# Entry of a gated delta net reordered, and its row scalings spread from DRAM

## The reference

```
q = l2_normalize(q) * 128 ** -0.5;  k = l2_normalize(k)
gcum  = cumsum(g)                                  # in a chunk
decay = exp(gcum_i - gcum_j), causal
m     = strict(k_beta k^T * decay)
u, w  = solve(I + m, [v * beta, k_beta * exp(gcum)])
attn  = (q k^T) * decay
q_dec = q * exp(gcum)                              # the row scaling of the queries
for each chunk:  v_new = u - w S;  o = q_dec S + attn v_new
                 S = S * exp(g_last) + k_dec^T v_new
```

## Time and profile before

| | before |
|---|---|
| runs (us) | 1338.09, 1340.19, 1348.91 |
| median | 1340.19 |
| profiled execution | 1343.36, span 1341.6 |
| PE busy | 1304.7 us, 97% of the span |
| DVE, ACT, POOL busy | 64%, 51%, 22% |
| mean granted TensorE clock | 0.991 |
| chain that ended last, by engine | PE 77%, DVE 10%, ACT 5% |

### The profile page before, as it was taken

How to read it: one execution, slowest core, us unless ns; L and a number is a source line. 1 busy time by engine, 2 the same in 40 slices (tenths; PEclk the granted TensorE clock), 3 DMA queues, 4 the chain that set the end, 5 groups by cost and what they waited for, 6 DMA issues and landing times.

```text
span 1341.6 us, 27229 instructions
## 1 busy us (share of the span) xinstructions
PE 1304.7 (97%) x10946; PEld 1226.9 (91%) x10946; DVE 859.0 (64%) x1271; ACT 681.5 (51%) x1098; POOL 290.8 (22%) x368
## 2 busy tenths in 40 slices
PE   6999999999799999999999999999999999999998
PEld 4899999997688888999999999999999988999998
DVE  4754789995457666533677656666736666875663
ACT  4458888866555554322534212343236665664553
POOL 3000223412587897513000000000130000200002
PEclk8999999999899999999999999999999999999999
DMA  9722323244231111123466566565423321556662
GB/s 325 209 80 81 94 79 95 80 114 151 98 111 33 49 48 33 64 95 110 146 202 196 181 193 195 183 197 178 129 95 126 97 69 32 182 173 220 190 201 80
DMA packets 138926, 174.90 MB, mean 130 GB/s; under 512 B 11025, under 2 KB 121873, under 8 KB 138561
## 3 DMA queue, kind: packets, MB, share of 16 engines
q1 hardware_dynamic: 137312, 168.94, 39.9%
q10 hardware_dynamic: 896, 4.23, 0.9%
q0 software_dynamic: 608, 0.19, 0.1%
HBM read 172.25 MB, written 1.08 MB: 129 GB/s over the span
## 4 chain that ended last, share of the span: by engine, by line
PE 77%; DVE 10%; ACT 5%; issue 3%; POOL 2%; DMA 1%; SPq 0%; ACTq 0%; DVEq 0%; POOLq 0%
PE bank L2728 54%; PE bank L2736 4%; DVE w_lo L1778 3%; DVE qkv L1864 2%; PE bank L3132 2%; PE bank L3141 2%; ACT w_hi L951 1%; PE bank L2654 1%; POOL qkv L806 1%; PE bank L3087 1%; PE bank L3408 1%; PE bank L3431 1%; DMA first_w<-in_w_mod 1%; PE bank L3006 1%; PE bank L3074 1%
## 5 line engine op out<-in xcount | busy, mean ns | idle before, releaser
L1778 DVE TENSOR_TENSOR w_lo<-raw,w_hi 128x1024 fp32r<-128x1024 f32 x212 | 264.2, 1247 | 297.1 <-ACT w_hi L951 296.6
L951 ACT ACTIVATE w_hi<-raw 128x1024 fp32r<-128x1024 f32 x212 | 223.9, 1057 | 379.9 <-PE bank L2728 371.8
L2728 PE MATMUL bank<-h_hi,w_hi 128*128 128x256 f32 x1472 | 299.4, 282 | 5.4 <-DVE w_lo L1778 2.9
L2728 PE MATMUL bank<-h_hi,w_lo 128*128 128x256 f32 x1472 | 293.7, 278 | 0.0
L2728 PE MATMUL bank<-h_lo,w_hi 128*128 128x256 f32 x1472 | 288.3, 278 | 0.0
L2728 PEld LDWEIGHTS bank<-h_hi,w_hi 128*128 128x128 f32 x1472 | 225.8, 189 | 15.5 <-issue 10.0
L2728 PEld LDWEIGHTS bank<-h_hi,w_lo 128*128 128x128 f32 x1472 | 225.7, 189 | 0.0
L2728 PEld LDWEIGHTS bank<-h_lo,w_hi 128*128 128x128 f32 x1472 | 222.6, 188 | 0.3 <-DVE h_lo L2076 0.2
L2728 PE MATMUL bank<-hid_hi,w_hi 128*128 128x256 f32 x768 | 172.0, 278 | 0.0
L2728 PE MATMUL bank<-hid_lo,w_hi 128*128 128x256 f32 x768 | 170.8, 277 | 0.0
L2728 PE MATMUL bank<-hid_hi,w_lo 128*128 128x256 f32 x768 | 170.7, 277 | 0.0
(11 more groups left out here) (380 smaller groups left out, 2445.3 us busy)
## 6 DMA issues: line engine op xcount, KB each, us to landing
raw<-in_mlp_w SPq DMA_DIRECT2D x128, 512.0 KB, 3.6
late_w<-in_w_mod SPq DMA_DIRECT2D x56, 512.0 KB, 4.4
raw<-in_even_w_in SPq DMA_DIRECT2D x48, 512.0 KB, 3.7
raw<-in_w_mod SPq DMA_DIRECT2D x24, 512.0 KB, 4.3
first_w<-in_w_mod SPq DMA_DIRECT2D x16, 512.0 KB, 11.2
raw<-in_even_w_out SPq DMA_DIRECT2D x16, 512.0 KB, 3.5
raw<-in_attn_w_qkv SPq DMA_DIRECT2D x16, 512.0 KB, 3.5
raw<-in_attn_w_o SPq DMA_DIRECT2D x8, 512.0 KB, 3.5
```

Source lines behind the costliest of these rows:

```text
L951: act.activation(stored(w_hi, j, four), raw[:, j % RAW], ACT.Copy).then_inc(hi_ready, 1)
L1778: dve.tensor_tensor(stored(w_lo, j, four), raw[:, j % RAW], stored(w_hi, j, four).bitcast(F32), ALU.subtract).then_inc(split_done, 1)
L2728: return pe.matmul(bank[2 * pair + t][:, c - n0:c - n0 + CTX], w_[:, k, t * P:(t + 1) * P], x_[:, c:c + CTX], start=(kk == 0 and first and ...
```

## The change

The row scalings come from a DRAM scratch. In body 8 ACT also writes exp of the gate sums of all steps to `eg_tok`, PE turns it (one transpose of 128 by 64), ACT copies the 64 by 128 result and stores it to `eg_rows`. ACT then loads, for each step, two transfers that put four rows of 128 on all partitions of `d_qd`. PE's and ACT's `rows` are gone, `log_gates` waits for `decay` (`p_dc`) instead, `decayed_q` for the transfers. The scratch of `eg_tok` and `eg_row` shares memory with `near`, hence the wait for `s_egw` there.

The entry is reordered: DVE leaves the wait for the silu of body 8's second pair until after `l2_scaled(1)`, and the split of unit 2 goes behind that; ACT loads group 2 before it takes the root of group 3, with the table load ahead of `neighbours`; PE starts step 0 when group 2 is scaled, not group 3; `decay(1)` moves ahead of the first doubling; DVE's split of an output unit in step 0 goes behind `neighbours(1)`.

```diff
@@ POOL
             def log_gates(q, d):
                 if q:
-                    pool.wait_ge(p_row, 2 * q - d)
+                    pool.wait_ge(p_dc, q)
...
             def decayed_q(q):
-                pool.wait_ge(a_row, 2 * q + 2)
+                pool.wait_ge(s_eg, 32 * (q + 1))
@@ ACT, the last two bodies of the input projection
                 if ends:
+                    act.preload_act_table_set("natural_log_exp_and_others")
                     neighbours(0)
-                    act.preload_act_table_set("natural_log_exp_and_others")
+                    l2_load(2)
                     l2_rstd(3)
-                    l2_load(2)
...
                     act.preload_act_table_set("silu_and_others")
                     evac(s, it, 1)
-                    act.preload_act_table_set("natural_log_exp_and_others")
...
                     l2_rstd(0)
                     act.wait_ge(s_gps, 3)
+                    eg_ = bank[X2][:, 0:64].rearrange("p (n d h) -> p n d h", d=2, h=8)
+                    for d in range(2):
+                        for cp in range(2):
...
+                            act.activation(y_, x_.rearrange("p c (g a) -> p g c a", a=2), ACT.Exp)
...
                     l2_rstd(1)
+                    act.wait_ge(s_gps, 4)
+                    act.activation(eg_row[0:8 * STEPS, :], bank[X0][0:8 * STEPS, 0:P], ACT.Copy).then_inc(s_gate, 1)
+                    act.wait_ge(s_gate, 7)
+                    act.dma_start(eg_dram[:, :], eg_row[0:8 * STEPS, :]).then_inc(s_egw, 16)
                     betas(0)
                     decay(0)
                     l2_load(1)
@@ ACT, the delta net
-            def rows(q, d):
-
-                act.wait_ge(p_row, 2 * q + 2 - d)
-                if q >= 2:
-                    act.wait_ge(p_os, q - 1)
-                act.activation(flat(d_qd[q % 2][:, d]), bank[R0][:, :], ACT.Exp).then_inc(a_row, 1)
...
+            def row_loads(q):
+                if q == 0:
+                    act.wait_ge(s_egw, 16)
+                    act.wait_ge(act_evac, 16)
+                else:
+                    act.wait_ge(g_qd, q)
+                if q >= 2:
+                    act.wait_ge(p_os, q - 1)
+                for d in range(2):
+                    r_ = 8 * q + 4 * d
+                    act.dma_start(d_qd[q % 2][:, d].rearrange("p i x -> p (i x)"),
+                                  eg_dram[r_:r_ + 4, :].rearrange("r x -> (r x)").partition_broadcast(P)).then_inc(s_eg, 16)
+
             flipped(0, -1, 0)
-            rows(0, 0)
             flipped(0, -1, 1)
+            act.preload_act_table_set("natural_log_exp_and_others")
+            row_loads(0)
             for q in range(STEPS):
...
                 gathered(q, 2, 1)
                 if prep:
-                    rows(q + 1, 1)
+                    row_loads(q + 1)
...
@@ DVE, entry and step 0
                     for part in range(3):
                         neighbours(0, part)
+                    l2_scaled(1)
+                    evac(s, it - 1, 1)
                     split_lo(u + 2, 2)
-                    l2_scaled(1)
...
-                evac(s, it, 1)
+                if b != LRU_TILES:
+                    evac(s, it, 1)
...
                 scores(q)
-                if q == 0:
-                    split_lo(SEG["out"]["unit"] + 1, 1)
                 masked(q, 2, 0)
                 reduced(q, 1, 1)
                 if prep:
                     neighbours(q + 1, 1)
                     neighbours(q + 1, 2)
+                if q == 0:
+                    split_lo(SEG["out"]["unit"] + 1, 1)
@@ PE
-            def rows(q, d):
...
-                for g_ in (d_gu, d_gl):
-                    mm = pe.matmul(bank[R0][:, :], lines[:, 2], flat(g_[:, d]), start=g_ is d_gu, stop=g_ is d_gl)
-                mm.then_inc(p_row, 1)
...
                     if g == 1:
                         pe.wait_ge(s_gate, 6)
+                        pe.wait_ge(l2["rs"], 1)
+                        pe.transpose(bank[X0][0:8 * STEPS, 0:P], eg_tok[:, :], C("ident")).then_inc(s_gps, 1)
                         decay(0)
...
-            pe.wait_ge(l2["out"], L2_OUT[3])
+            pe.wait_ge(l2["out"], L2_OUT[2])
...
-                if prep and q:
+                if prep:
                     decay(q + 1)
...
-                if prep and q == 0:
-                    decay(1)
...
                 second_product(q, 2, 1)
-                if prep:
-                    rows(q + 1, 1)
...
                 flip(q, 2, 1)
-                if prep:
-                    rows(q + 1, 0)
```

More of the change, by code:

```diff
@@ L3168, in l2_sums @@
                 pe.wait_ge(l2["sq"], 2 * g + 2)
+                if g == 2:
+                    pe.wait_ge(s_gate, 7)
                 if g >= 2:
@@ L3225, in _ @@
             first_product(0, 0, 0)
-            rows(0, 1)
             flip(0, -1, 0)
-            rows(0, 0)
             for q in range(STEPS):
```

21 lines of the change are left out of this document (12 added, 9 removed).

## The result

Over 20 runs each, the changed kernel takes 1335.91 us (1333.47 to 1343.31) and the kernel before 1344.8 us (1338.09 to 1349.99): a ratio of 0.9936, interval 0.9923 to 0.9948, or 8.6 us less (7.0 to 10.4). Faster, within 1%, as forecast to be likeliest; but the gain is smaller than the forecast 13.1 us, and 1335.91 lies just above the range of 1321 to 1335.

A forecast was written before the change was run, and what follows sets the result against it. The prediction took a chain of waits to bound the entry, and PE and an equally long circle through other engines the steps: 10.7 + 1.3 + 1.1 = 13.1 us off 1340.19, giving 1327.1 us, range 1321 to 1335.

The forecast's parts named there:

- The entry: Before step 1's decays: a chain of waits shortened by the new order, decays at 341.9 instead of 351.00, 9.1 us.
- the 2.9 taken: Entry: time assumed for POOL's pair of `d_t`, between 2.48 and 4.31 us in earlier rows.
- The 3.7: Entry: `d_t` time if DVE's lock on the shared port blocks POOL for one split; the sum would fall by 0.8 us.
- Step 0: From step 1's decays to `spread(1)`: further gains of 1.1 and 0.5 us, making 10.7 us with the entry.
- the split: Step 0: DVE's 1.57 us split moved behind the work for which PE waited, 1.1 us.
- PE's slow stretch at 359.55: Step 0: PE's 1.22 us there would become the 0.70 of a later step, 0.5 us.
- The steps: Row products removed from PE: 1.3 us in three even steps plus 1.1 in the last, 2.4 of 7.7 us.
- the last step: Last of the steps: no gates to write and no next decay, so its row products count in full, 1.1 us.
- Late transfers: Rival: POOL's copy of `d_last` waits for slow loads; gain gone at 12.4 us landing, 1353 at 14.4; chance 0.04.
- The rival with all row products: Rival in the steps: all 7.7 us of row products count, 18.4 us in total, 1321.8; chance 0.12.
- The filler's weights: Step 0: weight piece 3 waits for the moved split; PE may stand up to 1.6 us, taken as 0, bounds 0 and 0.5.
- the clock could take gain: Rival in the steps: PE's granted clock falls from 2.4 to 1.2 GHz; 26 us of it eats the gain; chance 0.03.

The follow-up runs named there:

- p_after: The changed kernel run again unaltered, as the measure for other runs of its call; ratio to the kernel before 0.9938 (0.9922 to 0.9954).
- c_dummy1: The changed kernel with matmuls of the row products' size and number put back on PE, 1.1 us per step; ratio to the kernel before 0.9937.
- e_spread: The changed kernel with one of seven levels of GpSimd's `spread` left out in steps 1 to 7; ratio to the kernel before 0.9888.
- d_dummy2: The changed kernel with twice the row products' matmuls put back on PE, 2.2 us per step; ratio to the kernel before 0.9962.

## Why the prediction came out as it did

- **The entry: right.** Counted from the first gates less the 1.54 us, the reduction came at 311.4 (forecast 311.6), `neighbours(0)` at 319.3 without a wait (319.7), `d_t` at 330.1 (330.1), the decays at 341.7 (341.9). That VectorE waits for the silu, not the load, was as forecast. GpSimd's `d_t` took 3.46 us, not the 2.9 taken, and nothing was late for it. The 3.7 that the prediction estimated by the rule of the Trainium skill (SBUF — State Buffer, section SBUF: two separate sides) was the nearer.
- **Step 0: right at full clock.** p_after gives 10.68 us at `spread(1)` (75.29 less 64.61), forecast 10.7, and term by term: 9.14 up to the decays (9.1), 1.02 from there to `neighbours(1)` (1.1 for the split), 0.52 from there to `spread(1)` (0.5 for PE's slow stretch at 359.55). The first trace gives 9.07. What failed there is a term put at nothing: that PE would run at the full clock behind the new wait after `z`. It ran slow there in five of six traces, and that cost 0.8 to 1.8 us. Before, such a stretch was over ahead of the decays. That one trace hits the forecast to 0.02 us is luck.
- **The steps: wrong, 2.4 us forecast, 0.1 measured.** The step that failed is the sentence that the next wait is that of `k_k` for ScalarE's decays. Between the row products and `k_k` stands `flip(q, LAST, 0)`, which issues `first_product` of the next step, and that needs `spread(q + 1)`. PE started it 0.14 to 0.17 us after the end of `d_t` in every step before, and 0.14 after. So PE came no earlier to `k_k`, and what it was late there in the even steps stayed (0.73, 0.35 and 0.37 us). For the last step I gave the full 1.1 us with the reason that no gates follow; `spread(7)` was still ahead of PE. c_dummy1 shows that PE's time was covered, e_spread by what.
- **The rivals.** Late transfers did not come: `d_last` does not wait in any step, though a transfer took up to 8.9 us to land (median 4.2). The rival with all row products took PE's 25.99 of 26 us as a bound; c_dummy1 and d_dummy2 refute it. The filler's weights, taken as 0, made PE wait 0.69 and 0.62 us in the first step after, and the step was no longer for it (24.03 us, 24.57 before). That the clock could take gain was named, but placed in the steps and given 3%; it was in step 0.
- **The base.** The three runs shown had a median of 1340.19; 20 have 1344.8. From there the forecast sum gives 1331.7. Of the 8.8 us between 1327.1 and 1335.91, 4.6 are the base; the rest is the steps (2.3) and the clock in step 0 (1.6 in the first trace), which is 3.9 of 4.2. This is an account by one trace: what the last section tells of PE's pace moves an execution by more.

## What to carry to other kernels

Before work is taken off an engine that looks full, read what its next instruction *of any kind* waits for, also where no bracket shows. If its start follows the end of its input at the same short distance in every step (here 0.14 us), the input sets the start, and the work ahead of it is covered. Put the work back as dummies of the same size: if the time stays, something else bounds the stage. A cut in that something (here one level of `spread`, or two copies ahead of a wait) then pays nearly one to one. Idle time of GpSimd was free in these traces only where VectorE idled too.

## What the runs showed of the hardware

PE's matmuls of 256 columns ran at one of two paces at the same granted clock of 1.00, in whichever kernel. Windows in the last stage of the first trace of the changed kernel and of p_after, the same program:

```profile
1220.00:1260.00 40.00, 40.00 (x356) 40.00 (x355) 24.34 (x32) 18.29 (x26) 0.00 (x0) 1.00 0.62 188
```

```profile
1220.00:1260.00 40.00, 40.00 (x342) 40.00 (x341) 22.20 (x29) 18.91 (x27) 0.00 (x0) 1.00 0.58 184
```

356 matmuls in 40 us against 342, without a wait in either: from start to start, 113 ns against 118. From `neighbours(7)` to the end it is 828.0 us in the one and 833.9 in the other, more than half of the change's whole gain. In all eighteen traces this distance is 828.0 to 829.4 us or 832.9 to 833.9, nothing between. The same two paces are found side by side in the input projection of one trace; that this makes the first gates stand anywhere from 286.2 to 290.2 us is likely, but not shown. What sets the pace was not found. For a change of under 1%, distances between two rows of one stage tell more than the medians do.
